# Layer 1's 24 weight-sum transfers issued at panel counts 178 to 249 instead of 182 to 280

## The reference

```
for i in range(2):
    mem_kv = rmsnorm(mem, mem_norm[i]) @ w_mem_kv[i]
    proj = rmsnorm(h, norm_mix_pre[i]) @ (ssd_w_in, swa_w_in)[i]
    y_mix = (ssd_mixer, swa_sink_attention)[i](proj, ...)      # layer 1: 16 query heads, 4 key/value heads
    y_mem = memory_cross_attention(proj[..., -512:], mem_kv)
    h = h + rmsnorm(concat(y_mix, y_mem) @ w_out[i], norm_mix_post[i])
    f = square(relu(rmsnorm(h, norm_mlp_pre[i]) @ w_up[i])) @ w_down[i]      # D_FF = 4096
    h = h + rmsnorm(f, norm_mlp_post[i])
```

## Time and profile before

| | |
|---|---|
| median of three runs | 1268.05 us (1267.55 to 1270.74) |
| the profiled execution | 1267.74 us, its span 1266.0 us |
| granted TensorE clock | 0.999 of full speed |
| PE busy | 1257.6 us, 99% of the span |
| DVE, ACT, POOL busy | 923.9, 754.2, 163.8 us |
| SP's queue q1 | 159.93 MB, 38.5% of 16 engines' span |
| POOL's queue q0 | 67.11 MB, 24.3% of 16 engines' span |

### The profile page before, as it was taken

The page is one execution under the profiler, slowest core; times in us unless marked ns, Lnnn a source line. Parts: engine busy times, 40 slices in busy tenths (PEclk is TensorE's granted clock), DMA queues, the critical chain, the costliest instruction groups (busy, mean ns, idle before and its releaser), DMA issues.

```text
span 1266.0 us, 19581 instructions
## 1 busy us (share of the span) xinstructions
PE 1257.6 (99%) x7655; PEld 1087.2 (86%) x7655; DVE 923.9 (73%) x1261; ACT 754.2 (60%) x1277; POOL 163.8 (13%) x195
## 2 busy tenths in 40 slices
PE   9999999999999999999999999999999999999998
PEld 7787878888888989999888898778889999988886
DVE  5676776899743686777787974877577776868886
ACT  6645355687652655567565753777564566665663
POOL 0046345363000000000000000000000000000000
PEclk9999999999999999999999999999999999999999
DMA  8488876352585357948876527656227378579754
GB/s 278 147 271 270 242 168 176 107 172 86 144 214 142 112 221 210 219 154 222 256 250 190 195 74 171 129 124 151 84 69 237 134 179 232 191 207 281 235 176 158
DMA packets 110531, 230.29 MB, mean 182 GB/s; under 512 B 8151, under 2 KB 18919, under 8 KB 110183
## 3 DMA queue, kind: packets, MB, share of 16 engines
q1 hardware_dynamic: 84384, 159.93, 38.5%
q0 software_dynamic: 21760, 67.11, 24.3%
q10 hardware_dynamic: 4294, 2.00, 0.8%
HBM read 225.69 MB, written 70.04 MB: 234 GB/s over the span
## 4 chain that ended last, share of the span: by engine, by line
PE 97%; ACT 1%; DVE 1%; DMA 0%; issue 0%; SPq 0%; DVEq 0%; ACTq 0%
PE G L2400 33%; PE G L2896 5%; PE G L2900 5%; PE G L2898 5%; PE X L2859 4%; PE X L2857 4%; PE X L2855 4%; PE X L2423 4%; PE X L2896 3%; PE X L2900 3%; PE X L2898 3%; PE X L2485 3%; PE G L2485 3%; PE G L2859 3%; PE G L2857 3%; PE G L2855 3%
## 5 line engine op out<-in xcount | busy, mean ns | idle before, releaser
L1388 ACT ACTIVATE whi<-raw 128x1024 fp32r<-128x1024 f32 x112 | 118.1, 1058 | 107.2 <-PE G L2900 33.7
L2152 DVE TENSOR_TENSOR wlo<-raw,whi 128x1024 fp32r<-128x1024 f32 x112 | 135.0, 1220 | 48.7 <-ACT whi L1388 48.1
L1588 DVE TENSOR_TENSOR wlo<-raw,whi 128x1024 fp32r<-128x1024 f32 x77 | 94.6, 1229 | 80.9 <-ACT whi L873 80.7
L1306 ACT ACTIVATE whi<-raw 128x1024 fp32r<-128x1024 f32 x84 | 88.8, 1060 | 103.0 <-PE X L2859 52.6
L2400 PE MATMUL G<-uhi,whi 128*128 128x512 f32 x352 | 144.8, 411 | 0.2 <-DVE ulo L1605 0.2
L2085 DVE TENSOR_TENSOR wlo<-raw,whi 128x1024 fp32r<-128x1024 f32 x84 | 102.6, 1222 | 58.1 <-ACT whi L1306 57.6
L2400 PE MATMUL G<-uhi,wlo 128*128 128x512 f32 x352 | 137.7, 391 | 0.0
L2400 PE MATMUL G<-ulo,whi 128*128 128x512 f32 x352 | 137.3, 390 | 0.0
L873 ACT ACTIVATE whi<-raw 128x1024 fp32r<-128x1024 f32 x77 | 81.5, 1058 | 80.1 <-PE G L2400 30.0
L775 POOL DMA_DIRECT2D tsum<-in_w_down x32 | 32.9, 1039 | 619.3 <-PE G L2400 326.6
L2896 PE MATMUL G<-whi,left_hi 128*128 128x512 f32 x224 | 87.1, 389 | 0.0
(11 more groups left out here) (455 smaller groups left out, 3687.4 us busy)
## 6 DMA issues: line engine op xcount, KB each, us to landing
tsum<-in_w_down POOLq DMA_DIRECT2D x48, 1024.0 KB, 10.1
raw<-in_w_up SPq DMA_DIRECT2D x64, 512.0 KB, 5.8
raw<-tsum SPq DMA_DIRECT2D x64, 512.0 KB, 4.1
raw<-in_w_down SPq DMA_DIRECT2D x48, 512.0 KB, 5.1
raw<-in_ssd_w_out SPq DMA_DIRECT2D x16, 512.0 KB, 4.6
raw<-in_swa_w_in SPq DMA_DIRECT2D x16, 512.0 KB, 4.2
csrow<-cs_rows SPq DMA_DIRECT2D x16, 384.0 KB, 4.7
raw<-in_swa_w_out SPq DMA_DIRECT2D x12, 512.0 KB, 3.9
```

Of the source, the lines that this page charges most:

```text
L1306: act.activation(whi[n % 4][:, :, :], up_right(g, r, q), ACT.Copy).then_inc(hi_done, up_fill(g, k))
L1388: act.activation(whi[n % 4][:, :, :], down_raw[n % 4][:, :, :], ACT.Copy).then_inc(hi_done, 1)
L1588: dve.tensor_tensor(wlo[q][:, :, :], src[:, :, :], whi[q][:, :, :].bitcast(F32), ALU.subtract).then_inc(lo_done, 1)
L2152: dve.tensor_tensor(wlo[n % 4][:, :, :], down_raw[n % 4][:, :, :], whi[n % 4][:, :, :].bitcast(F32), ALU.subtract).then_inc(lo_done, 1)
```

## The change

Only the table changes: the count of finished panels at which each transfer of layer 1 is issued. The transfers, their order and their number (24) stay.

```diff
-W1_SUM_AT = tuple(range(182, 196, 2)) + (208, 210) + tuple(range(213, 257, 4)) + (262, 268, 274, 280)
+W1_SUM_AT = tuple(range(178, 202, 2)) + (208, 210) + tuple(range(213, 253, 4))
```

## The result

The changed kernel takes 1274.73 us, the median of 6 runs (1274.12 to 1277.16), the kernel before 1267.80 us in as many (1267.34 to 1270.74). The medians lie 6.9 us apart (0.55%). The ratio estimated from all twelve runs is 1.0048, with a 95% interval of 1.0037 to 1.0060 (two of the six runs before took 1270.6 and 1270.7 us). The change is clear of noise, in the direction the forecast gave and beyond its range (1269.2 us forecast, up to 1273.0). It comes near the price of rival (b), 1274.5 us. By the bound of 0.3% the outcome is "slower", to which 0.12 was given.

A forecast was written before the change was run, and what follows sets the result against it. PE, busy 1257.6 of 1266.0 us, is paced by its own products. 1267.74 + 0 + 0 + 0 + 1.2 = 1268.9 us profiled, 1269.2 with 0.3 up to the median; range 1266.9 to 1273.0.

The forecast's parts named there:

- rival (b): In front of attention: three late panel loads reach PE through the softmax; 1274.5 us at 10.5 each; 0.12 beyond 3.8 us.
- term 1: Down phase: four adding transfers go away and ACT's waits shrink, but PE's products keep their pace, 0 us.
- terms 2 and 3: Up phase: 0 us, 1 us either way as bounds; output projection: three copies beside its loads, 0 us.
- The issue times of 758.5, 764.3 and 775.2: In front of attention: predicted starts of the adding transfers at counts 178, 180 and 182.
- The chain up to ACT: In front of attention: late loads of 183 and 184 delay the load of 186; its rounding slips 2.7 to 5 us.
- Rival (d): POOL also waits for earlier transfers on the same rows; time as in (a); 0.39 together with (a).
- (a): In front of attention: loads keep to 5 us and prepared panels swallow it; 1268.05 us; 0.39 together with (d).
- (c): Down phase: loads there held PE back now and then; 3 to 5 us come back, 1264; chance 0.04.
- The step that failed: Start of block QB: ACT's query copies end at 786.7 to 789, PE wants the bank at 787.1; loss 0 to 1 us.
- another path, the softmax: In front of attention: late panel 187 delays DVE's first softmax step by 0 to 4 us; PE loses 0 to 2.6 us.
- The term that was mis-sized: In front of attention: a load beside an adding transfer lands after 9.2 us, bounds 3.9 and 13.4.
- What the prediction drew from the rule: In front of attention: queues served in turn would give loads their share at once, so nothing is lost; the forecast followed the row.

The follow-up runs named there:

- experiment 1: Changed kernel without its two earliest points (178, 180), n = 0 to 11 at 182 to 200, 204 and 206: 1269.38 us against 1268.60, ratio 0.9998.
- Experiment 7: Changed kernel's table, but ACT and DVE copy the queries of block QA before rounding panel 186: 1269.72 us, ratio 1.0012.
- experiment 2: Kernel before with only its first seven transfers moved, to 178 to 190, counts 208 to 280 kept: 1275.12 us, ratio 1.0049.
- experiment 4: Changed kernel's later points, but one early adding transfer at 178, none at 180, then 182 to 200 and 206: 1274.54 us, ratio 1.0042.
- experiment 5: Changed kernel with plain 1 MB copies in place of the adding transfers at 178 and 180: 1269.22 us, ratio 1.0023.
- 6: Changed kernel with both early transfers (178, 180) but none at 182, then 184 to 200 and 206: 1268.82 us, ratio 1.0006.
- 8: Changed kernel's table, only DVE copies its queries (banks 0 and 3) before its part of panel 186: 1270.17 us, ratio 1.0024.
- experiment 3: Changed kernel's later points, but one early adding transfer at 180, none at 178 (180 to 200, then 206): 1268.27 us, ratio 0.9994.

## Why the prediction was wrong

**What held.** That nothing is won in the down phase (term 1), that up phase and output projection cost nothing (terms 2 and 3), within noise: experiment 1 and the windows. That the whole effect sits in front of the attention, starts with the loads of panels 183 and 184, and is kept to the end. The issue times of 758.5, 764.3 and 775.2 were measured as

```profile
758.26 1.01 POOL L775 DMA_DIRECT2D tsum<-in_w_down  x1 [150.22 <-PE X L2485]
764.02 1.01 POOL L775 DMA_DIRECT2D tsum<-in_w_down  x1 [4.75 <-PE X L2485]
774.93 1.01 POOL L775 DMA_DIRECT2D tsum<-in_w_down  x1 [9.89 <-PE G L2400]
```

The chain up to ACT had the right order and was short by 1.0 to 1.4 us of what came: load 184 was to land at 771.6 to 774 and landed at 775.37; load 186 was to go out at 774 to 776.3 and land at 783.2 to 785.5, it went out at 777.74 and landed at 786.52. Rival (d) did not come; (a) and (c) fell.

**The step that failed** is the one behind it: "Behind it on ACT stand the query copies [...] PE wants the first of these banks one bank [...] into block QB [...]: at 785.8 + 1.3 = 787.1 [...]. Loss of PE: 0 to 1 us." I followed banks 1 and 2, which ACT copies, and left out that DVE copies banks 0 and 3 (L2262) with its rest of panel 186 in front of them. DVE's timeline of the kernel before already showed the order:

```profile
781.54 1.23 DVE L1588 TENSOR_TENSOR wlo<-raw,whi 128x1024 fp32r<-128x1024 f32 x1 [4.21 <-ACT whi L873]
782.68 1.38 DVE L2262 COPY qT<-G 64x512 f32<-64x512 f32 x2
```

Bank 0 is wanted first, at 785.4 in the changed kernel, and it is free later than both of ACT's banks, whose copies end at 789.90: landing 786.5, ACT's rounding 1.07, DVE's rest 1.24, two copies to 790.16. With the landings of 783.2 to 785.5 that stood in the prediction, the same sum gives 1.5 to 3.8 us of waiting instead of 0 to 1. Rival (b) named the place and nearly the time, but by luck: it asked for three landings of 10.5 us each (panels 183, 185 and 187), where 183 took 10.0 and 185 5.7, and it took another path, the softmax, which costs nothing here, since PE itself is late by then. Experiment 7 shows that path as the next in line, with 2.0 us. The prediction also read the 2.7 us of the earlier trace rows as waits of PE for the softmax; they are waits of PEld, and PE has none for the softmax in the earlier trace rows.

**The term that was missing** is TensorE's clock. I priced a wait of PE at its own length. The waits of 4.2 to 6.3 us in the changed kernel and experiments 2, 4 and 5 came with steps of 6.1 to 7.9 us, and in each of these four profiles the granted clock was down: the lowest window of 4 us has 0.50 in the changed kernel and in experiment 2, 0.54 in experiment 4 and 0.75 in experiment 5. Those of 1.0, 2.0 and 2.2 us (6, 7 and 8) came with steps of 1.2, 2.1 and 2.45, and with 1.00 in every window of 4 us from 784 to 800.

**The term that was mis-sized** is the range of a load beside an adding transfer. I took 9.2 us as if it were one size per load. Those of 183 and 184, one behind the other with two copies of V in a third queue, took 10.0 and 11.7. More important, the price depends on order: 7.3 us for a load that is 7.6 us behind an adding transfer (experiment 3), 8.8 to 10.4 for one that is 0.9 to 3.6 us behind (the changed kernel, 4, 5, 7, 8), 3.7 with none in front (6). A delay of 5.8 us in its issue moved the load of 186 from in front of a transfer to behind one, and so became 9.8 us of landing (776.7 to 786.52).

**The load beside the transfer.** The Trainium skill ("DMA: Bandwidth & Descriptors", Queues, rings and completion order) has the queues served in turn. The rows of 761 to 767 us above say again what the earlier trace rows said: the load that is already issued gets nothing from 761 to 764 (97.8% for q0), as before the change from 777 to 781 (100.3%). Both stretches end some 5.8 us after the issue of the adding transfer (758.26 and 775.21); then the load gets its share (30.8% of the engines beside 78.7%, over the whole 3 us). What the prediction drew from the rule, that nothing would be lost, did not come.

## What to carry to other kernels

Where a bulk transfer is given an earlier start, look up for each load in the next stretch on which side of a bulk transfer's issue it falls, and by how few microseconds: a small slip that puts it behind one can cost much more than itself (here a landing of 4.8 us became one of 8.8 to 10.4). Then follow the late load along each engine that works in order, to the last thing that stands behind it and not only to the panel itself; panel 186 itself was ready 17 us before PE wanted it (782.8 against 799.6 in the kernel before), bank 0 behind it only 1.6 (784.06 against 785.63). And price a wait of the matmul engine with what its clock loses after it.

## What the runs showed of the hardware that I had not expected

A wait of 4.8 us in front of block QB brought a granted clock of 0.50, which began within the wait and held for products that ran at 0.43 us instead of 0.23, some 1.9 us on top; waits of 1.0, 2.0 and 2.2 us did not. And two kernels whose tables differ in one number, 180 against 178 for the first transfer, are 1268.27 and 1274.54 us, while the one with two plain copies in that place (experiment 5) has times near both.
